# The second norm's token factors by way of DRAM instead of two passes with ones, in a one-core encoder layer

## The reference

```
h  = RMSNorm(x)
P  = h @ W_in                      # 1024 -> 6656 columns
A, B, C = two attentions and a pooling on parts of P
x  = x + (sig(g_A)*(A W_a) + sig(g_B)*(B W_b) + sig(g_C)*(C W_c)) @ W_out
h2 = RMSNorm(x)                    # x * r(token) * gain(channel)
u  = h2 @ W_up                     # 1024 -> 5632 columns
c  = causal depthwise convolution of width 3 over the tokens of u, plus a bias
x  = x + (silu(c[gate half]) * c[value half]) @ W_down
```

## Time and profile before

| | |
|---|---|
| median of 3 runs | 815.77 us (815.57 to 817.28) |
| the profiled execution's own time | 817.54 us |
| its span | 815.9 us |
| PE (TensorE matmuls) busy | 809.2 us |
| PEld (TensorE weight loads) busy | 670.8 us |
| DVE busy | 639.0 us |
| ACT busy | 418.6 us |
| POOL busy | 23.5 us |
| DMA | 115.37 MB, mean 141 GB/s |

### The profile page before, as it was taken

The page is one execution under the profiler, slowest core; times in us unless marked ns, Lnnn a source line. Parts: engine busy times, 40 slices in busy tenths (PEclk is TensorE's granted clock), DMA queues, the critical chain, the costliest instruction groups (busy, mean ns, idle before and its releaser), DMA issues.

```text
span 815.9 us, 11415 instructions
## 1 busy us (share of the span) xinstructions
PE 809.2 (99%) x3808; PEld 670.8 (82%) x3808; DVE 639.0 (78%) x944; ACT 418.6 (51%) x587; POOL 23.5 (3%) x38
## 2 busy tenths in 40 slices
PE   8999999999999999999999999999999999999998
PEld 6888888888888888888888888888888888888886
DVE  4958888868678676577788968777777888898797
ACT  5655776665546554435346464433433344566653
POOL 0010010000000050000000000000000000000000
PEclk9999999999999999999999999999999999999999
DMA  6243232222222224265547322666565555576455
GB/s 212 86 124 99 81 105 78 84 71 78 77 77 59 83 78 133 87 206 185 180 138 233 99 75 86 205 206 195 190 203 187 183 181 195 165 218 210 149 183 173
DMA packets 131071, 115.37 MB, mean 141 GB/s; under 512 B 6260, under 2 KB 109656, under 8 KB 129888
## 3 DMA queue, kind: packets, MB, share of 16 engines
q1 hardware_dynamic: 130048, 112.47, 43.9%
q0 software_dynamic: 672, 2.12, 0.9%
q10 hardware_dynamic: 320, 0.40, 0.2%
HBM read 101.31 MB, written 13.65 MB: 141 GB/s over the span
## 4 chain that ended last, share of the span: by engine, by line
PE 98%; DMA 1%; DVE 0%; SPq 0%; issue 0%; DVEq 0%
PE ps L1841 30%; PE ps L1843 30%; PE ps L1842 30%; PE ps L1963 2%; PE ps L1954 2%; PE ps L1978 1%; PE ps L1977 1%; DMA x_in<-in_x_dram 1%; PE ps L1878 1%; PE ps L2159 0%; DVE out_sb L1826 0%; PE ps L1937 0%; PE ps L1938 0%; SPq L356 0%; DVE out_sb L1832 0%
## 5 line engine op out<-in xcount | busy, mean ns | idle before, releaser
L1841 PE MATMUL ps<-h_lo,w_hi 128*128 128x512 f32 x704 | 276.8, 393 | 0.0
L1842 PE MATMUL ps<-h_hi,w_hi 128*128 128x512 f32 x704 | 274.1, 389 | 0.0
L1843 PE MATMUL ps<-h_hi,w_lo 128*128 128x512 f32 x704 | 274.1, 389 | 0.0
L1110 DVE TENSOR_TENSOR w_lo<-w_raw,w_hi 128x1024 fp32r<-128x1024 f32 x104 | 128.2, 1233 | 68.1 <-ACT w_hi L620 33.8
L1843 PEld LDWEIGHTS ps<-h_hi,w_lo 128*128 128x128 f32 x704 | 132.1, 188 | 27.9
L1841 PEld LDWEIGHTS ps<-h_lo,w_hi 128*128 128x128 f32 x704 | 132.2, 188 | 27.6 <-DVE h_lo L1641 0.3
L1842 PEld LDWEIGHTS ps<-h_hi,w_hi 128*128 128x128 f32 x704 | 132.3, 188 | 26.4
L620 ACT ACTIVATE w_hi<-w_raw 128x1024 fp32r<-128x1024 f32 x72 | 76.3, 1059 | 139.6 <-PE ps L1843 139.5
L614 ACT ACTIVATE w_hi<-w_raw 128x1024 fp32r<-128x1024 f32 x32 | 33.9, 1060 | 62.7 <-PE ps L1843 59.4
L1689 DVE TENSOR_TENSOR conv_in<-ps,r_ffn 128x512 f32<-128x512 f32 x44 | 30.3, 689 | 22.5 <-PE ps L1843 22.2
L1029 ACT ACTIVATE conv_out<-conv_in,par 128x512 f32<-128x512 f32 x44 | 35.5, 806 | 9.6 <-DVE conv_in L1689 9.6
(11 more groups left out here) (283 smaller groups left out, 1360.1 us busy)
## 6 DMA issues: line engine op xcount, KB each, us to landing
w_raw<-in_w_in_dram SPq DMA_DIRECT2D x103, 256.0 KB, 3.2
w_raw<-in_w_up_dram SPq DMA_DIRECT2D x88, 256.0 KB, 3.2
raw_t<-in_w_down_dram SPq DMA_DIRECT2D x9, 1024.0 KB, 8.9
down_sums<-t_sum SPq DMA_DIRECT2D x9, 1024.0 KB, 5.7
w_raw<-in_w_down_dram SPq DMA_DIRECT2D x33, 256.0 KB, 3.0
w_raw<-down_sums SPq DMA_DIRECT2D x33, 256.0 KB, 3.8
raw_o<-in_w_out_dram SPq DMA_DIRECT2D x6, 512.0 KB, 4.8
w_raw<-down_sums SPq DMA_DIRECT2D x22, 128.0 KB, 2.9
```

The lines of the kernel that those rows point to most:

```text
L1110: v.tensor_tensor(w_lo[:, slot, :], w_raw[:, slot, :], r32(w_hi[:, slot, :]), ALU.subtract)\
L1841: mm3(dst, l_hi, r_lo, start=start, stop=False, **kw)
L1842: mm3(dst, l_hi, r_hi, start=False, stop=False, **kw)
L1843: return mm3(dst, l_lo, r_hi, start=False, stop=stop, **kw)
```

## The change

The diagonals, the two matmuls of ones and ACT's copy are gone. GpSimd's queue waits for the factors, stores them as 512 words in token order in a DRAM tensor, waits for that store, and loads them from there, with a step of zero over the partitions, straight into `r_ffn`. DVE waits for this transfer in place of ACT's copy. Unit N_UP + 3 (tile 4) is split by ACT and DVE ahead of the first product instead of behind it.

```diff
-        sq_x1, r_hi, r_lo = region(132, ("sq_x1", [P, D], FP32), ("r_hi", [P, TT, P], F32R), ("r_lo", [P, TT, P], F32R))
+        sq_x1, = region(132, ("sq_x1", [P, D], FP32))
...
+        r_dram = nc.dram_tensor("token_factors", (S,), FP32, kind="Internal").ap()
...
@@ gpsimd, at its end
+            pool.wait_ge(ffn_step, 4)
+            pool.dma_start(r_dram.rearrange("(t p) -> p t", p=P), tok[:, 5, :], allow_slow_non_contiguous=True).then_inc(r_stored, 16)
+            pool.wait_ge(r_stored, 16)
+            pool.dma_start(r_ffn[:, :], bass.AP(r_dram.tensor, 0, [[0, P], [1, S]])).then_inc(r_landed, 16)
@@ scalar
             a.preload_act_table(ACT.Silu)
             hi(N_UP + 2, 0)
-            a.wait_ge(r_in_psum, 1)
-            act(r_ffn[:, :], ps[:, 4, :], ACT.Copy).then_inc(r_ready, 1)
+            hi(N_UP + 3, 1)
...
-                        elif not (first and e in (0, 2)):
+                        elif not (first and e < 3):
                             hi_at(n + gv + 2, gv, jj * 2 + (N_UP // 2 + i + 1))
@@ vector
-            d.wait_ge(ffn_step, 4)
-            for t in range(TT):
-                last = v.tensor_scalar(r_hi[:, t, :], ident[:, :], tok[:, 5, t:t + 1], None, ALU.mult)
-            last.then_inc(ffn_step, 1)
-            d.wait_ge(ffn_step, 5)
-            for t in range(TT):
-                last = v.scalar_tensor_tensor(out=r_lo[:, t, :], in0=ident[:, :], scalar=tok[:, 5, t:t + 1],
-                                              in1=r32(r_hi[:, t, :]), op0=ALU.mult, op1=ALU.subtract)
-            last.then_inc(diag_ready, 1)
             v.memset(conv_in[:, :, 0:2], 0.0).then_inc(cin_zero, 1)
             lo(N_UP + 2, 0)
-            d.wait_ge(r_ready, 1)
+            lo(N_UP + 3, 1)
+            d.wait_ge(r_landed, 16)
             d.wait_ge(cin_zero, 1)
...
                 conv_input(0, 0, 0)
-                lo(N_UP + 3, 1)
                 conv_input(0, 0, 1)
@@ tensor
-            def spread_r():
-
-                pe.wait_ge(diag_ready, 1)
-                mm3(ps[:, 4, :], ones_all[:, :], r_lo[:, :, :], start=True, stop=False)
-                mm3(ps[:, 4, :], ones_all[:, :], r_hi[:, :, :], start=False, stop=True).then_inc(r_in_psum, 1)
...
-                                midway=spread_r if first and e == 1 else None, midway_at=KD - 1,
```

More of the change, by code:

```diff
@@ L253, in build @@
                                                      sem("h2_lo"))
-        x1_ssq, x1_ln, x1_exp, ffn_step, diag_ready, r_in_psum, r_ready = (
-            sem("x1_ssq"), sem("x1_ln"), sem("x1_exp"), sem("ffn_step"), sem("diag_ready"), sem("r_in_psum"),
-            sem("r_ready"))
+        x1_ssq, x1_ln, x1_exp, ffn_step = sem("x1_ssq"), sem("x1_ln"), sem("x1_exp"), sem("ffn_step")
+        r_stored, r_landed = sem("r_stored"), sem("r_landed")
         cin_zero, cin_ready, tap_init, tap1_done, conv_done = (sem("cin_zero"), sem("cin_ready"), sem("tap_init"),
```

## The result

The changed kernel takes 824.37 us, median of 6 runs (823.59 to 825.25), where the kernel before takes 815.72 (6 runs, 815.57 to 817.50): ratio 1.0105, 95% interval 1.0095 to 1.0115. That is 8.65 us slower, outside the predicted range. The profiled execution took 825.25, its span is 823.5; it is the slowest of the six.

What follows compares the result with a forecast made beforehand. The prediction took TensorE, busy 99% of the span, to bound the kernel. A gain of 0.20 us and a stall of 0.35 gave +0.15 on the median 815.77: 815.9 us, range 815.1 to 818.0.

Steps and rivals of the forecast that it cites:

- Where to look, and the paths: TensorE's stream at the up-projection's start: two matmuls (0.54 us) go, but tile 3 waits for its split; gain 0.20 us.
- What moves: Tile 4's weights are split before the first product, costing nothing; SP's load for tile 6 goes out 1.9 us sooner.
- The wake-ups: Fixed part of the DMA chain: 0.28 us twice for POOL, 0.1 for DVE, from 475.49 to 476.15.
- The store, a: POOL's store of 512 single words to DRAM: 3.6 us taken, 2.6 below, 5.6 above.
- signs of being wrong: A store over 5 us, an issue over 1 us, TensorE waiting at another tile, or a change elsewhere in the kernel.
- The broadcast, b: POOL's load of 2 KB from DRAM to 128 partitions (256 KB): 4.0 us taken, 5.0 above.
- Who waits for that: From the first product on: tile 5 isn't held; tile 6 starts at S + 11.67 or 495.07, whichever is later; stall 0.35.
- S: Start of DVE's first product (conv_in): forecast 483.75, ends 482.1 and 486.8, against 479.04 before.
- The sum: Gain of 0.20 at tile 3 against a stall of 0.35 before tile 6: net +0.15 us, 815.9.
- Slow store: Rival: the 512 words are generated and drained one by one; net over 1.6 us, 818.4 at +2.65; chance 0.14.
- Held issue: Rival: the broadcast's issue waits for DVE's split, 1.2 us more, S = 484.95, net +1.35, 817.1; chance 0.06.
- Covered: Rival: the two DMAs take 3.3 + 3.3 or so, S under 483.4, only the 0.20 gain left, 815.57; chance 0.21.

Runs made afterwards that it cites:

- the kernel with the wait filled: The changed kernel with 30 matmuls without use between tile 4 and tile 5, in TensorE's wait: 823.75 us, ratio 1.0100 to the kernel before.
- the words in partition order: The kernel before plus a store of 512 single words nothing waits for, each partition's 4 words side by side in DRAM: 817.57 us, ratio 1.0025.

## Why the prediction was wrong, step by step

- **Where to look, and the paths.** Right. The two matmuls are gone, tile 3 is held by its split (0.47 and 0.50 us on its weight load), and DVE's order from the first product on decides. I gave a gain of 0.20; the distance from the factors to tile 3 fell from 3.42 to 3.09, so it is 0.3: the split ended where I put it, but TensorE followed it by 0.05 us, not 0.19. Neither can be told from nothing: with no factor at all the ratio is 0.9999.
- **"What moves".** Right: the moved split alone measures 0.9999. The sooner load for tile 6 did share the DMA engines, but with the store, and took 9.3 us for 3.1; what it did to the store and the broadcast in turn no run separates.
- **The wake-ups.** Right: 0.29 twice for POOL, and none to speak of for DVE; I had 0.28, 0.28 and 0.1.
- **The store, a.** This is the step that failed: "I take 3.6", and above, 5.6. It measured 9.8. My bounds went by the number of words, in the issue (1.6 more; it grew by 0.2, to 0.77) and in the drain (1.4 more, for 32 packets per engine; the profile has two per engine on average from GpSimd's queue, 0.19 us in all). Both were the wrong quantity: 512 words take 2.2 us when each has 64 bytes to itself, and 128 words take 8.6 when they are neighbours. The 20 KB store was no neighbour of this one in kind, since it writes rows of 2560 bytes. Two of my own signs of being wrong came: a store over 5 us, and TensorE's wait at another tile.
- **The broadcast, b.** 5.9 for 4.0, above my 5.0. It ran beside the loads that the store had held up, with the engines' share at 1.11 in 486 to 488. With the 16-byte store it took 4.2. It also slowed as the row that it re-reads got shorter and the reads more: 6.4 for 256 reads of 1 KB, 10.4 for 512 of 512 bytes, though other loads were late there too; I have not separated the two.
- **"Who waits for that."** The formula held and the number put into it did not. In the profile before's time S is 491.77; S + 11.67 gives 503.44. Tile 5, which I had as not held, starts at S + 4.51 (I had 4.66 from S for its start) and is the first to wait. Measured on the same scale: tile 6 at 504.65. The rest, 1.2 us, is the clock, a term that my sum put at nothing: I had no wait long enough for it to matter. In the kernel with the wait filled S + 11.53 is measured.
- **The sum.** 6.2 us for a and 1.9 for b put S 8.0 later than forecast; 0.35 of stall was already in the forecast. -0.20 + 0.35 + 8.0 + 1.2 = 9.35, and the profiled execution has 9.38. The median lost 8.65: the profiled execution is 0.9 above it, and its mean granted clock is the lowest of the six, 0.994 against 0.996.
- **The rivals.** "Slow store" named the place, the side and the reason to fear, with a chance of 0.14, but priced it by the word and so stopped at 818.4. "Held issue" is refuted where it could be seen: in the kernel with 16-byte pieces the broadcast's issue at 475.44 falls beside DVE's split at 474.85 to 476.08 and takes 0.54 as ever. That agrees with the Trainium skill's SBUF — State Buffer (Who interferes with whom) on the shared port pair, by which a DVE operation with two SBUF inputs stands only in the way of a GpSimd operation that reads SBUF. "Covered" is what the 16-byte pieces give, S some 6.6 us after the factors, 815.45. There the store's 1.8 agrees with the fixed 2.0 us of the Trainium skill's DMA: Bandwidth & Descriptors (Anatomy of one DMA, SWDGE path); the broadcast's 256 KB took 4.2, where that fit gives an estimate of 2.6, and the words side by side took 9.8, where it gives 2.0. The measurements decide.
- **A price that I didn't give at all**: what the store does to others. It alone, waited for by nobody, costs 3.7 us. I had asked what the loads would do to the broadcast, not what 2 KB would do to the loads. The 3.7 alone is more than the 0.3 us that the removal can bring.

## What to carry to other kernels

Before sending a column over DRAM, look at what lands beside what: 512 single words side by side took over four times as long as the same words 64 bytes apart and held back SP's loads meanwhile, while the column stored as it lies, 16 bytes per partition, and reordered on the reading side landed in 1.8 us. Where an operation has no row in the trace, one far bound from rows of another kind is no bound. The change could win 0.3 us, so the unknown's far end, and what it does to the transfers beside it, should have weighed more than its middle.

## What the runs showed of the hardware that I had not expected

- 512 single words in token order: 9.6 to 9.9 us from GpSimd's queue and 10.2 from SP's; in places of 64 or of 512 bytes: 2.2; 256 words side by side: 10.6; 128: 8.6. From 128 to 512 words the time hardly depends on their number.
- The store's packets are on record in the first 2 us behind its issue, whether it lands after 2.2 us or after 9.6.
- During such a store SP's loads of 256 KB took 7.3 to 10.1 us instead of 3.1 to 3.2, on another queue than the store's (8.0 and 5.6 beside the words in partition order).
- GpSimd's issue took 0.77 us for 512 pieces, 0.73 for 256 and 0.55 for 128; the count was not what cost.
- A stall of 6.5 us let the granted clock fall to the lower level within it, and it stayed there for the first 14 matmuls of tile 5, up to 500.6; most of that was hidden by DVE's own chain.
